# Hybrid decoder layer on one core: the turned tiles of B and x finished apart from their transposition, and the transpositions and stores gathered once a group

## The chip, the cores and the metric

One Trainium2 chip, one of its cores. The time is the device time of one execution in microseconds; of several executions the median is given. The profile is one further execution, taken by the hardware profiler.

## What is computed

A decoder layer with a state-space mixer over 2048 tokens of 1024 features (16 learned tokens stand ahead of them), all in float32:

```python
h = concat([meta, x])
proj = rms_norm(h, norm_mix_w) @ w_in                # [u | z | x B C | dt], 5144 columns
y_pool = pool_mixer(u)                               # 4 trailing means, then a linear map
xbc = silu(causal_dwconv(xBC, conv_w, conv_b))       # 4 taps for each channel
# 24 heads of 64 in 4 groups of 6; B and C (128) are shared by the heads of a group
# in chunks of 128 tokens, S the state that a head carries from chunk to chunk:
y  = ((C B^T) * decay) (x dt) + exp(a_cs) * C S + d_skip * x
S  = S * exp(a_last) + B^T (exp(a_last - a_cs) * x dt)
y  = rms_norm_of_group(y * silu(z)) * ssm_norm_w
h  = h + concat([y_pool, y]) @ w_out
h  = h + relu(rms_norm(h) @ w_ff1)**2 @ w_ff2
out = rms_norm(h, norm_f_w)[:, 16:]
```

## The kernel before

**Blocks.** The 2048 tokens go through the mixer in four blocks b = 0 to 3 of 512 tokens (4 chunks of 128). Block 0 also splits the weights into a high and a low part and stores them; the blocks 1 to 3 load them. After the mixer of a block comes its down projection (line 2031), and after all four the feed-forward part, which makes up the second half of the span. Every product is made of three products of high and low parts.

**The program of each engine** is written out by hand, in order, and engines meet on semaphores alone. In the blocks 1 to 3 the mixer's input products are items: for each group g, B, C, three tiles of x (j = 0, 1, 2, 3, 4: units of 128 columns by 512 tokens, line 1924), then four pieces of the gate z (one for each chunk, 384 columns, line 2011). The items of group 0 come first. Then come 16 steps q = 4 g + c; the step works on chunk c of group g and, between its parts, TensorE makes the items of group g + 1: `mixer_plan` (line 714) gives item n1 at the start of a step and the items n2 later in it, three items in the fourth step and two in the others. The steps of group 3 have no n1 and, from the group's first, one item of the pooling part. So the third step of a group (c = 2) has the last x tile as n1 and the first gate piece as n2, and the fourth (c = 3) has three gate pieces.

**An item** goes from TensorE's bank v % 2 to ScalarE, which evacuates it (`evac`, line 1395, lines 1412 and 1413 for a gate piece; it waits until item v - 2 is finished), to VectorE's taps (line 2467), ScalarE's tanh (line 1447), and VectorE's `finish` (line 2474). TensorE's item v waits until item v - 2 is evacuated (line 1994).

**A step on TensorE** (from line 2207): item n1, transpositions of y of q - 2 (line 2104), diagonal product of q - 1 (line 2116), `slot1` of q (lines 2078 and 2084), state product of q - 1 (line 2134), items n2, and y_offset of q (line 2096). The state product waits for yo of q - 1 on VectorE.

**A step on VectorE** (from line 2642): y of q - 1 (`y_finish`, lines 2565 and 2567), state addition of q - 1 (`state_add`, line 2575), taps of n1, mask (2659), the decay product (2676), B's low part (2682), xdt and xw (2688, 2692), y's low part (2588), xw's low part (2580), the finishes of the pending item and of n1, yo (2705), taps of n2.

**A step on ScalarE** (from line 1597): evacuation of n1, tanh of the pending item, c_both (1608), six falls (1615), the state's high part (1508; in group 3 later), exponential (1621), B's high part (1633), in group 0 the copy of the tokens (1641), squares of y (1534), y's high part (1502), tanh of n1, scaling of y (1518, after GpSimd's root, 1149), xw's high part (1513), evacuation of the items n2. **GpSimd**: low parts of C and of the state (1181, 1185), the root (1148, 1149), ty (1193), the state's carry (1196), ty plus yo (1205).

**Turned tiles.** In group 0 TensorE turns B and x from features by tokens to tokens by features itself (line 2078). For the groups 1 to 3 of the blocks 1 to 3, VectorE turns squares of 32 by 32 within the tile at the end of `finish` (line 2510): B from its tile into `b_turn`, x from `pre` into its own place in F. `store_turned` (line 1385), called at the end of each `evac` for item v - 2, stores the tile to `xt_scr` in HBM, and SP's `load_tokens` (line 846, issues of line 856) brings it back with the squares in their places. F holds two groups' tiles in turn (`group_tile`, line 302).

**SP's queue** (from line 875): for each unit n the weights, 4 units ahead; between them the sums, and at given n the loads of turned tiles and, at n = 16 and 24, the stores of the normalized h of the block before (`store_turned_h`, line 836, four DMAs for each tile t of 128 tokens).

## Time and profile before

| what | us |
| --- | --- |
| median of 3 executions | 2657.96 |
| lowest and highest | 2656.44, 2659.02 |
| the profiled execution | 2655.4 |
| its span | 2653.7 |
| TensorE busy | 2630.8 |
| VectorE, ScalarE, GpSimd busy | 1674.7, 1241.4, 1110.9 |

In the rows PE is TensorE, PEld its weight loads, DVE VectorE, ACT ScalarE, POOL GpSimd, SP the engine that issues most DMAs; ACTq and SPq are the queues' own issues. An operation is named by its line, what it writes and what it reads. A bracket tells how long the engine was idle before it and whose end released it. Times are from the start of the span. The ends of matmuls are modelled, so one overlaps the next; the distance from start to start is what they cost. The granted clock is that of TensorE, 1.00 is 2.4 GHz.

### The profile page before, as it was taken

The page shows a single profiled execution, that of the slowest core. Times are in us where ns is not written, and L with a number is a line of the kernel's source. Part 1 is how long each engine was busy: PE and PEld are TensorE (multiplying, and loading weights), DVE is VectorE, ACT ScalarE, POOL GpSimd, SP SyncE. Part 2 cuts the span into 40 slices and gives each one's busy share as a digit, 9 for nine tenths or more (in the row PEclk, how much of TensorE's full clock was granted, in tenths as well). Part 3 has the DMA queues.
Part 4 walks back from the last instruction along what each step waited for, and adds up shares of the span by engine and source line. Part 5 has one row for each costly group of instructions (what it writes and reads, how often), then busy time and mean ns, then how long its engine had stood idle before and what let it go on. Part 6 is the DMA issues. An engine that isn't in the chain of part 4 may idle for free.

```text
span 2653.7 us, 37407 instructions
## 1 busy us (share of the span) xinstructions
PE 2630.8 (99%) x13818; PEld 2199.1 (83%) x13818; DVE 1674.7 (63%) x2264; ACT 1241.4 (47%) x2474; POOL 1110.9 (42%) x866
## 2 busy tenths in 40 slices
PE   8999999999999999999999999999999999999998
PEld 6888788888888888888888888888888888888887
DVE  6788715888157882478853576564445766666667
ACT  4667653666236662356724455554544222222223
POOL 2133440345004450034544688665555435353434
PEclk9999999999999999999999999999999999999999
DMA  9977676886548866579773655764446742423324
GB/s 333 306 258 244 236 250 247 242 244 220 215 184 264 245 193 235 198 228 253 215 273 138 212 203 198 265 246 142 164 138 236 282 152 101 159 96 127 119 95 159
DMA packets 372739, 551.58 MB, mean 208 GB/s; under 512 B 139450, under 2 KB 240830, under 8 KB 364494
## 3 DMA queue, kind: packets, MB, share of 16 engines
q1 hardware_dynamic: 353550, 539.75, 60.1%
q10 hardware_dynamic: 19008, 9.44, 1.2%
q8 instruction: 110, 1.80, 0.3%
q14 instruction: 71, 0.58, 0.1%
HBM read 393.75 MB, written 155.39 MB: 207 GB/s over the span
## 4 chain that ended last, share of the span: by engine, by line
PE 52%; DVE 1%; DMA 1%; issue 1%; ACT 0%; POOL 0%; SPq 0%; POOLq 0%; ACTq 0%; DVEq 0%
PE bank L2337 22%; PE bank L2305 22%; PE bank L2031 3%; PE bank L1924 3%; PE bank L2011 1%; DMA pair_raw<-T_scr 1%; DVE stage L2812 0%; PE bank L2116 0%; PE bank L2134 0%; PE bank L2096 0%; DVE T_lo L2829 0%; PE bank L2084 0%; PE bank L2104 0%; PE bank L2050 0%; DVE T_lo L2819 0%
## 5 line engine op out<-in xcount | busy, mean ns | idle before, releaser
L1924 PE MATMUL bank<-hnT_hi,w_ring 128*128 128x512 f32 x1152 | 367.6, 391 | 1.6 <-ACT acc L1413 1.6
L2337 PE MATMUL bank<-w_first,T_hi 128*128 128x512 f32 x896 | 275.8, 389 | 0.0
L1924 PEld LDWEIGHTS bank<-hnT_hi,w_ring 128*128 128x128 f32 x1152 | 216.2, 188 | 47.6 <-ACT acc L1413 2.6
L2467 DVE SCALAR_TENSOR_TENSOR acc<-pre,par,acc 128x512 f32<-128x512 f32 x240 | 203.1, 846 | 79.2 <-ACT pre L1428 73.5
L2847 DVE TENSOR_TENSOR acc_th<-bank,acc_th 128x512 f32<-128x512 f32 x224 | 149.9, 685 | 154.1 <-PE bank L2337 153.2
L2305 PE MATMUL bank<-T_hi,w_both 128*128 128x512 f32 x768 | 242.5, 389 | 0.5 <-DVE ff L2788 0.5
L2031 PE MATMUL bank<-w_ring,T_hi 128*128 128x512 f32 x768 | 238.7, 392 | 0.0
L1924 PE MATMUL bank<-hnT_lo,w_ring 128*128 128x512 f32 x576 | 224.5, 390 | 0.0
L2337 PEld LDWEIGHTS bank<-w_first,T_hi 128*128 128x128 f32 x896 | 168.2, 188 | 34.9
L2011 PE MATMUL bank<-w_ring,hnT_hi 128*128 128x384 f32 x768 | 195.9, 335 | 0.6 <-DMA w_ring<-w_scr 0.6
L1924 PE MATMUL bank<-hnT_hi,w_both 128*128 128x512 f32 x544 | 181.9, 405 | 0.2 <-ACT pre L1428 0.2
L2305 PE MATMUL bank<-b,w_both 128*128 128x512 f32 x768 | 179.5, 389 | 0.1
L2337 PE MATMUL bank<-T_hi 128*128 128x512 f32 x448 | 174.4, 389 | 0.6 <-DVE T_lo L2829 0.6
L2337 PE MATMUL bank<-T_hi,T_lo 128*128 128x512 f32 x448 | 174.3, 389 | 0.0
L2337 PE MATMUL bank<-T_lo,T_hi 128*128 128x512 f32 x448 | 174.3, 389 | 0.0
L2337 PE MATMUL bank<-w_first,T_lo 128*128 128x512 f32 x448 | 174.3, 389 | 0.0
L2305 PEld LDWEIGHTS bank<-T_hi,w_both 128*128 128x128 f32 x768 | 144.2, 188 | 31.3 <-DVE ff L2788 1.3
L2305 PEld LDWEIGHTS bank<-b,w_both 128*128 128x128 f32 x768 | 144.0, 188 | 30.3 <-DVE ff L2780 0.5
L2031 PEld LDWEIGHTS bank<-w_ring,T_hi 128*128 128x128 f32 x768 | 142.8, 188 | 28.7
L2305 PE MATMUL bank<-hnT_hi,w_both 128*128 128x512 f32 x512 | 163.2, 389 | 0.0
L1264 POOL TENSOR_TENSOR w_both<-w_sum,w_both 128x512 fp32r<-128x512 f32 x64 | 86.9, 1358 | 181.1 <-ACT w_both L1722 181.1
L1722 ACT ACTIVATE w_both<-w_sum 128x512 fp32r<-128x512 f32 x128 | 80.8, 631 | 173.0 <-PE bank L2305 139.3
(320 smaller groups left out, 6243.1 us busy)
## 6 DMA issues: line engine op xcount, KB each, us to landing
w_ring<-w_scr SPq DMA_DIRECT2D x312, 512.0 KB, 4.7
T_scr<-stage SPq DMA_DIRECT2D x32, 1792.0 KB, 6.6
w_scr<-w_both SPq DMA_DIRECT2D x100, 512.0 KB, 4.3
pair_raw<-in_w_ff SPq DMA_DIRECT2D x36, 1024.0 KB, 5.5
third<-T_scr SPq DMA_DIRECT2D x28, 1024.0 KB, 4.9
pair_raw<-T_scr SPq DMA_DIRECT2D x28, 1024.0 KB, 4.8
sums<-sums_scr SPq DMA_DIRECT2D x64, 384.0 KB, 5.3
raw<-in_w_in SPq DMA_DIRECT2D x36, 512.0 KB, 6.4
```

The source lines that it names most:

```text
L1264: nc.gpsimd.tensor_tensor(lo, left_source(g), hi.bitcast(F32), ALU.subtract).then_inc(w1_lo_pool, 1)
L1722: nc.scalar.activation(hi, left_source(g), ACT.Copy).then_inc(w1_hi, 1)
L1924: mm = nc.tensor.matmul(bank[s][:, :], w[:, k, :], t[:, k, :], start=(k == 0 and j == 0), stop=(k == KT - 1 and j == 2))
L2011: mm = nc.tensor.matmul(bank[s][:, 0:GW].rearrange("p (u c) -> p u c", c=P), t[:, k, tok], w[:, k, :, :], start=(k == 0 and j == 0), stop= ...
L2031: mm = nc.tensor.matmul(bank[4 + t][:, :], a, w[:, kk, :], start=(u == 0 and kk == 0 and j == 0), stop=(u == 7 and kk == 1 and j == 2))
L2305: mm = nc.tensor.matmul(bank1(p, m), w[:, k, :], t[:, k, :], start=(m not in (2, 7, 3) and k == 0 and j == 0), stop=(m not in (1, 6, 5) an ...
L2337: mm = nc.tensor.matmul(bank[4 * half + t][:, :], a[:, k, tok], w[:, k, :], start=(SECOND[q % 7] not in GOES_ON and k == 0 and j == 0), st ...
L2467: ins = nc.vector.scalar_tensor_tensor(acc[:, s, 0:TB], pre[:, s, k:k + TB], w, acc[:, s, 0:TB], ALU.mult, ALU.add)
L2847: ins = nc.vector.tensor_tensor(dst, src, dst, ALU.add)
```

## The change

In the blocks 1 to 3, B's and x's tiles of the groups 1 to 3 are finished in one operation like all others. Their four transpositions stand in a row at the end of the third step of the group before (`x_turning`), in the order B, x, x, x; the turned x goes to the other half of F, where the tiles of the group in work are, and in group 0 waits until TensorE has turned these itself for the last time. The four stores stand in a row in the fourth step, ahead of c_both, each behind its transposition. In the blocks 1 to 3 the state addition stands ahead of y's two operations. The stores of h go out at n = 16 (t = 0, 1), 24 (t = 2) and 32 (t = 3), and y's high parts wait for them accordingly. The load of the next block's x also waits for y of step 14. Whole, but for the context of some parts:

```diff
@@ -314,7 +314,10 @@
         def turn_tile(g, j):
-            return b_turn if j == 0 else group_tile(g, j)
+            return b_turn if j == 0 else group_tile(g + 1, j)
+
+        TURNED = (0, 2, 3, 4)
+        H_STORED_AT = {16: (0, 2), 24: (2, 3), 32: (3, 4)}
         def x_by_pe(b, q):
             return b == 0 or q < CH
@@ -367,6 +370,7 @@
                        for c in range(CH)]
         b_stored = sig("b_stored", 16 * (GROUPS - 1), 0, 0)
         xt_stored = sig("xt_stored", 48 * (GROUPS - 1), 0, 0)
+        x_turned = sig("x_turned_then_w2_loaded2", len(TURNED) * (GROUPS - 1), 0, 0)
         xt_loaded = [sig(f"xt_then_w2_loaded{i}", 64 * (GROUPS - 1), 0, 0) for i in range(2)]
         zc_ps = sig("zc_ps", STEPS)
         z_late = sem("z_late")
@@ -413,7 +417,8 @@
         refill_loaded = [sem(f"refill_loaded{i}") for i in range(3)]
         refill_hi, refill_lo = sem("refill_hi"), sem("refill_lo")
         split_loaded = [sem(f"split_loaded{i}") for i in range(3)]
-        w2_loaded = [xt_loaded[i].sem if i < 2 else sem(f"w2_loaded{i}") for i in range(5)]
+        w2_loaded = [xt_loaded[0].sem, xt_loaded[1].sem, x_turned.sem, sem("w2_loaded3"),
+                     sem("w2_loaded4")]
         w2_sum_ready, w2_hi, w2_lo = sem("w2_sum_ready"), sem("w2_hi"), sem("w2_lo")
         t_loaded = [sem(f"t_loaded{i}") for i in range(2)]
         t_hi, t_lo = sem("t_hi"), sem("t_lo")
@@ -653,7 +658,7 @@
         def w2_arrived(l):
-            return 16 * (l // 5 + 1) + (64 * (GROUPS - 1) * (BLOCKS - 1) if l % 5 < 2 else 0)
+            return 16 * (l // 5 + 1) + (64, 64, len(TURNED), 0, 0)[l % 5] * (GROUPS - 1) * (BLOCKS - 1)
         def w2_source(q):
             c, i = divmod(q, 7)
@@ -898,10 +903,11 @@
                             done = g if j >= 5 else g - 1
                             if after is not None and 0 < done < GROUPS:
                                 load_sums(b, done, after)
-                        if b and n == 24:
-                            hT_stored.wait(sp, b - 1, 128)
-                        if b and n in (16, 24):
-                            for t in (0, 1) if n == 16 else (2, 3):
+                        if b and n in H_STORED_AT:
+                            first, after = H_STORED_AT[n]
+                            if first:
+                                hT_stored.wait(sp, b - 1, 64 * first)
+                            for t in range(first, after):
                                 store_turned_h(b - 1, t)
                         if b and g >= 2 and j == 0:
                             load_tokens(b, g - 1, 0)
@@ -916,6 +922,7 @@
                                 load_tokens(b, GROUPS - 1, 1)
                             if b < LAST and (d, i) == (0, 3):
                                 yoff_ps.wait(sp, b, STEPS)
+                                gated.wait(sp, b, STEPS - 1)
                                 sp.dma_start(xn, x_in[0, (b + 1) * TB:(b + 2) * TB, :].rearrange(
                                     "(t p) d -> p t d", p=P)).then_inc(next_loaded.sem, 16)
                             if (d, i) == (0, 4 if b else 6):
@@ -1382,12 +1389,10 @@
                 steps = Steps(act, act_sem)
-                def store_turned(b, v):
-
-                    n = unit_of(b, v) if b and v >= ITEMS_G else None
-                    if n is None or n >= U_POOL or n % UNITS_G not in (0, 2, 3, 4):
-                        return
-                    g, j = divmod(n, UNITS_G)
+                def store_turned(b, g, k):
+
+                    j = TURNED[k]
+                    x_turned.wait(act, b, len(TURNED) * (g - 1) + k + 1)
                     act.dma_start(xt_scr[b, g, :, j - 2 if j else 3].rearrange("c p n -> p c n"),
                                   turn_tile(g, j).rearrange("p (c n) -> p c n", n=P)
                                   ).then_inc(xt_stored.sem if j else b_stored.sem, 16)
@@ -1397,11 +1402,6 @@
                     s = v % 2
                     ps = bank[s][:, :]
                     up_out.wait(act, b, v - 1)
-                    evacuate(b, v, s, ps)
-                    store_turned(b, v - 2)
-
-                def evacuate(b, v, s, ps):
-
                     piece = piece_of(b, v)
                     if piece:
                         g, c = piece
@@ -1498,6 +1498,8 @@
                     if b and q == CH:
                         hT_stored.wait(act, b - 1, 128)
                     if b and q == 2 * CH:
+                        hT_stored.wait(act, b - 1, 192)
+                    if b and q == 3 * CH:
                         hT_stored.wait(act, b - 1, 64 * CH)
                     nc.scalar.activation(T_hi[:, 4 + 3 * g:7 + 3 * g, c * P:(c + 1) * P],
                                          bank[2][:, 0:GW].rearrange("p (i t) -> p i t", t=P),
@@ -1600,6 +1602,9 @@
                                 high_part(act, N0 + n1 + 2)
                             evac(b, n1)
                             tanh(b, pending)
+                            if b and c == CH - 1:
+                                for k in range(len(TURNED)):
+                                    store_turned(b, g + 1, k)
                         if b:
                             yoff_ps.wait(act, b, q)
@@ -2494,20 +2499,9 @@
                         g, j = divmod(n, UNITS_G)
                         if n >= UNITS_G and j == 0:
                             state_ps.wait(dve, b, (g - 1) * CH if g >= 2 else 0)
-                        if b == 0 or g == 0 or ct is None or j == 1:
-                            nc.vector.scalar_tensor_tensor(group_tile(g, j), pre[:, s, 0:TB], 1.0,
-                                                           acc[:, s, 0:TB], ALU.add, ALU.mult
-                                                           ).then_inc(up_out.sem, 1)
-                            return
-                        dst = group_tile(g, 0) if j == 0 else pre[:, s, 0:TB]
-                        steps.link(nc.vector.scalar_tensor_tensor(dst, pre[:, s, 0:TB], 1.0,
-                                                                  acc[:, s, 0:TB], ALU.add,
-                                                                  ALU.mult))
-                        if j == 0:
-                            sums_stored.wait(dve, b, 16 * GROUPS)
-                        if j == 0 and g > 1:
-                            b_stored.wait(dve, b, 16 * (g - 1))
-                        nc.vector.transpose(turn_tile(g, j), dst).then_inc(up_out.sem, 1)
+                        nc.vector.scalar_tensor_tensor(group_tile(g, j), pre[:, s, 0:TB], 1.0,
+                                                       acc[:, s, 0:TB], ALU.add, ALU.mult
+                                                       ).then_inc(up_out.sem, 1)
                         return
                     i = n - U_POOL
@@ -2539,6 +2533,18 @@
                         hnT_lo[:, k, :], bank[2 + k % 2][:, :],
                         par[:, W_NMIX + k:W_NMIX + k + 1], hnT_hi[:, k, :].bitcast(F32),
                         ALU.mult, ALU.subtract).then_inc(hn_lo.sem, 1)
+
+                def x_turning(b, g, k):
+
+                    j = TURNED[k]
+                    up_out.wait(dve, b, g * ITEMS_G + j + 1)
+                    if k == 0:
+                        sums_stored.wait(dve, b, 16 * GROUPS)
+                        if g > 1:
+                            b_stored.wait(dve, b, 16 * (g - 1))
+                    elif g == 1:
+                        xb_ps.wait(dve, b, CH)
+                    nc.vector.transpose(turn_tile(g, j), group_tile(g, j)).then_inc(x_turned.sem, 1)
                 def h_turning(b, t):
@@ -2660,8 +2666,11 @@
                         if b and n1 is None:
                             masked = mask()
+                        if b and q:
+                            state_add(b, q - 1)
                         if q:
                             y_finish(b, q - 1)
+                        if b == 0 and q:
                             state_add(b, q - 1)
                         taps(b, n1)
                         if b == 0 and n1 is not None:
@@ -2705,6 +2714,9 @@
                         nc.vector.tensor_tensor(by_head(yo[:, :]), by_head(bank[7][:, 0:GW]),
                                                 per_head(ea, c, g), ALU.mult
                                                 ).then_inc(yo_ready.sem, 1)
+                        if b and n1 is not None and c == CH - 2:
+                            for k in range(len(TURNED)):
+                                x_turning(b, g + 1, k)
                         if n1 is None and c >= 2:
                             finish(b, pending - 1)
                         if b == 0 and q < STEPS - 1:
```

## Rows read from the trace of the kernel before

**Rows 1.** The page: busy time of the engines
```profile
PE 2630.8 (99%) x13818; PEld 2199.1 (83%) x13818; DVE 1674.7 (63%) x2264; ACT 1241.4 (47%) x2474; POOL 1110.9 (42%) x866
```

**Rows 2.** Busy time by stretch, block 1's mixer (stretch, length, engines, PEclk, DMA, GB/s)
```profile
465.00:650.00 185.00, 183.87 (x1229) 162.01 (x1227) 152.90 (x249) 121.40 (x331) 88.21 (x106) 1.00 0.79 227
```

**Rows 3.** Waits of TensorE, 460 to 1300 us (total, times, longest)
```profile
PE bank L2134 <- DVE yo L2705: 1.8, 3, 0.6
PE bank L1924 <- ACT acc L1413: 1.6, 3, 0.6
```

**Rows 4.** Three lines of code, all instructions (ns: least/median/most; first, last start)
```profile
L2510 DVE STREAM_TRANSPOSE F<-pre x27: 711/711/716, 480.9 to 1288.9; 128x512 f32<-128x512 f32 x27
L2503 DVE SCALAR_TENSOR_TENSOR pre<-pre,acc x27: 647/678/1322, 480.1 to 1288.2; 128x512 f32<-128x512 f32 x27
L1205 POOL TENSOR_TENSOR ty<-ty,yo x64: 996/1440/1848, 105.8 to 1333.0; 128x384 f32<-128x384 f32 x64
```

**Rows 5.** Timeline of VectorE, block 1, group 0, third step (start, duration)
```profile
486.12 0.56 DVE L2575 TENSOR_TENSOR S<-bank,S 128x384 f32<-128x384 f32 x1 [0.19 <-PE bank L2134]
...
492.03 1.18 DVE L2692 TENSOR_TENSOR xw<-xt,dte 128x384 f32<-128x384 f32 x1
...
494.99 0.71 DVE L2510 STREAM_TRANSPOSE F<-pre 128x512 f32<-128x512 f32 x1
495.63 0.65 DVE L2503 SCALAR_TENSOR_TENSOR pre<-pre,acc 128x512 f32<-128x512 f32 x1
496.31 0.71 DVE L2510 STREAM_TRANSPOSE F<-pre 128x512 f32<-128x512 f32 x1
496.95 0.52 DVE L2705 TENSOR_TENSOR yo<-bank,ea 128x384 f32<-128x384 f32 x1
...
499.71 0.55 DVE L2575 TENSOR_TENSOR S<-bank,S 128x384 f32<-128x384 f32 x1
```

**Rows 6.** Timeline of ScalarE and its DMA queue, group 0, fourth step
```profile
497.06 0.37 ACTq L1391 DMA_DIRECT2D xt_scr<-F  x1
...
497.82 0.31 ACT L1608 ACTIVATE c_both<-F 128x128 fp32r<-128x128 f32 x1
...
500.30 0.52 ACT L1508 ACTIVATE s_both<-S 128x384 fp32r<-128x384 f32 x1 [0.43 <-DVE S L2575]
...
507.17 0.48 ACT L1413 ACTIVATE acc<-bank 128x384 f32<-128x384 f32 x1
```

**Rows 7.** Timeline of TensorE, group 0, third and fourth step
```profile
495.20 0.39 PE L2116 MATMUL bank<-xdt,E 128*64 128x64 f32 x6
...
507.71 0.50 PE L1924 MATMUL bank<-hnT_hi,w_ring 128*128 128x512 f32 x1 [0.54 <-ACT acc L1413]
```

**Rows 8.** Timelines of VectorE, ScalarE, TensorE, block 1, group 1, fourth step
```profile
552.41 0.52 DVE L2705 TENSOR_TENSOR yo<-bank,ea 128x384 f32<-128x384 f32 x1
...
553.27 0.31 ACT L1608 ACTIVATE c_both<-F 128x128 fp32r<-128x128 f32 x1
...
555.76 0.53 ACT L1508 ACTIVATE s_both<-S 128x384 fp32r<-128x384 f32 x1 [0.43 <-DVE S L2575]
...
561.90 0.49 ACT L1413 ACTIVATE acc<-bank 128x384 f32<-128x384 f32 x1
...
562.47 0.47 PE L1924 MATMUL bank<-hnT_hi,w_ring 128*128 128x512 f32 x1
```

**Rows 9.** Timelines of ScalarE and TensorE, block 1, group 2 to 3
```profile
617.74 0.33 ACT L1608 ACTIVATE c_both<-F 128x128 fp32r<-128x128 f32 x1
618.64 1.87 ACT L1615 ACTIVATE E<-sums,acs 128x128 f32<-128x128 f32 x6 [0.56 <-PE bank L2116]
...
624.65 0.60 ACT L1518 ACTIVATE y<-y,small 128x384 f32<-128x384 f32 x1
...
625.31 0.55 PE L2104 MATMUL bank<-ident,y 128*128 128x128 f32 x3
```

**Rows 10.** SP's issues of the loads of turned tiles (ns)
```profile
L856 SPq DMA_DIRECT2D xt<-xt_scr x72: 302/583/5375, 501.5 to 1314.9; - x72
```

## The prediction

> **What bounds the kernel now.** The page first: TensorE is busy 2630.8 us of a span of 2653.7 [rows 1]. The change touches the mixer of the blocks 1 to 3 alone, and the table by stretch shows that of block 1: in 185 us TensorE is busy 183.87 at a granted clock of 1.00, VectorE 152.9, ScalarE 121.4 [rows 2]. Blocks 2 and 3 show the same within 0.02 us. So nothing that makes VectorE's or ScalarE's work less is worth anything in itself. The time moves only where TensorE waits, or where it would newly wait. The list of waits has two such places, three times each, once a block: 0.6 us before the state product (line 2134) for VectorE's yo, and 0.54 us before an input unit (line 1924) for ScalarE's evacuation [rows 3]. With the pipeline's refill they cost about 0.84 and 0.70 us. All that the change could win is therefore 3 x 1.54 = 4.6 us, 0.17%. A measurement of this kernel tells about 0.2%, 5.3 us, from no change.
>
> **The pieces.** I count the mixer's steps from q = 0; four make a group. A transposition of 128x512 takes 0.71 us, a finishing operation 0.68, and 1.32 where it collides with GpSimd; GpSimd's ty takes 1.0 to 1.85 [rows 4].
>
> **1. The finishing operation and the transposition come apart.** The count of instructions stays (36 and 36). Only the wait between the two goes, some 0.04 us each. What moves are four transpositions a group: B's and the first x tile's out of steps with spare VectorE time, and two out of the third step, where they stand ahead of yo. In block 1, group 0 these start at 494.99 and (after 495.63) at 496.31, and yo starts at 496.95 [rows 5]. Start to start a transposition holds the engine 0.64 us (494.99 to 495.63), so yo comes 2 x 0.64 = 1.28 us earlier by this part.
>
> **2. State added first.** In the third step the state addition at 486.12 already waits 0.19 us for its product [rows 5], so it can't come earlier; the two operations of y, which filled that time, now come after it, and the taps and all behind them about 1.1 us later. In group 1 the addition could start some 0.1 earlier, so about 0.95. Against that, the shift takes VectorE partly out of GpSimd's way: nothing to 0.64 us comes back (the 1.32 less the 0.68 of rows 4). I take 0.6, since the slow row of group 1 ends with a GpSimd operation that doesn't move. So yo starts at 496.95 - 1.28 + 1.05 - 0.6 = 496.1. yo ended at 496.95 + 0.52 = 497.47 and TensorE had waited 0.6 us for it, so it was ready at 496.9; yo now ends at 496.6, and this wait is gone. Otherwise the displacement costs nothing: xw, which ended at 492.03 + 1.18 = 493.2, becomes 0.5 to 1.1 later, and TensorE takes it in the diagonal product at 495.20 [rows 7]; in the steps with taps no wait of rows 3 hangs on VectorE. If that margin of 0.9 us went, each us more would go to TensorE. In group 3 the exponential, on ScalarE, ends after y either way.
>
> **3. Four transpositions in a row.** They start about 0.45 us after yo and take 3 x 0.64 + 0.71 = 2.63 us: 496.6 to 499.2. In group 0 the second to fourth also wait for TensorE's own transpositions of the fourth step, whose last is read by about 496.9; B's goes first, to 497.2, and covers that. Behind them wait the state addition (499.71 before, now 499.2) and y. That is early enough.
>
> **4. Four stores in a row on ScalarE's queue, before it goes on.** Here I see the cost. ScalarE now waits for the fourth transposition and issues its store (0.37 us [rows 6]) before c_both, the falls, the exponential and all that depends on them. c_both started at 497.82; now at 499.2 + 0.04 + 0.37 + 0.05 = 499.65, 1.83 later. Of this, 0.43 us was an idle wait for the state addition (500.30) [rows 6], which isn't needed any more. 1.4 us are left, and from the exponential on the chain has no slack for TensorE: squares, GpSimd's root, y's scaling, xw's high part, VectorE's low part, the gate's finish, then the evacuation that ended at 507.17 + 0.48 = 507.65 [rows 6]. TensorE's unit started at 507.71, at once behind it, after a wait of 0.54 [rows 7]; the low part, the gate's finish and GpSimd's root keep their durations. So this start moves to about 509.1: **+1.4 us** net, with both old waits inside it, since an absolute time on ScalarE sets it.
>
> **5. The same in group 1.** yo was at 552.41; with 1.28 less, 0.95 more and 0.64 less it is at 551.45, the transpositions end at 554.5, c_both goes from 553.27 to 555.0, and less the 0.43 wait before 555.76 the chain is 1.3 late. Its evacuation ended at 561.90 + 0.49 = 562.39, and TensorE took it at 562.47 [rows 8]: 0.1 us of slack, where no list of waits shows anything yet. **+1.2 us.**
>
> **6. In group 2** the falls of the next step waited 0.56 us for TensorE anyway (618.64) [rows 9]. c_both at 617.74 + 1.3 = 619.04 puts the falls at 619.24, 0.6 late; y's scaling ended at 624.65 + 0.60 = 625.25 and TensorE took it at 625.31. **+0.5 us.**
>
> **7. The DMA queues.** SP's load of the turned tiles waits for the last store. It was issued at 497.06 and is now at 499.2, with two more ahead of it, and SP's weight loads queue behind those waits. Those wait for the two gate units behind which they stand in any case, and the tokens are first used a unit into the next group, so I take nothing; the cover is the fourth step of a group, and if the loads came later than that, ScalarE's B part would wait. The stores of h over three groups take four of SP's DMAs from n = 24 to n = 32; TensorE reads none of them: nothing, either way. The new wait for gated before the next block's x is met in the same step as, and ahead of, the one that stands there. GpSimd's queue gets no wait; its low parts of C and of the state come later with ScalarE's, still within the two gate units that TensorE has in that step.
>
> **Sum.** 1.4 + 1.2 + 0.5 = 3.1 us a block, 9.3 in three. The profiled execution took 2655.4 us (span 2653.7), so 2664.7 for it; its time is 2.6 us under the median of the runs, 2657.96, to which I add the same: **2667.3**. Bounds: if a store's issue doesn't hold ScalarE (0.37 less) and nothing is given back in part 2 (0.6 more) these nearly cancel; 0.8 us either way at three places in three blocks is 7 us, but not all on one side.
>
> A transposition that meets GpSimd is in no row: all 36 take 0.71. It could take up to 0.64 more, as the finishing operation does; I take nothing, the nearer case: all 36 lie within 5 ns of each other, where the finishing operation, with two inputs in SBUF, spreads from 0.65 to 1.32 [rows 4]. The Trainium skill (SBUF - State Buffer, "Who interferes with whom") says that a VectorE instruction with two SBUF inputs contends with GpSimd's reads; a transposition has one, and by that rule the sum stays.
>
> **Rivals.**
> - **ScalarE isn't held (0.15).** If the four stores are all out by 497.82 + 0.43 = 498.25, the chain starts no later than before. Then the first wait is gone, the state is ready 0.5 us earlier, and the second goes too: -1.54 a block, 2657.96 - 4.6 = 2653.4. This is the case on the other side of no change. It needs the last transposition done by 497.85, 1.35 us before my figure, which two transpositions fewer would give. For it speaks that ScalarE also gets its two evacuations of the third and fourth step 1 us sooner; against it that it has nothing to do with that time but wait.
> - **A milder form (0.20).** The batch ends some 0.7 us earlier than I have it, through GpSimd's collisions, or ScalarE catches up: +0.6, +0.5 and 0 a block: +3.3, 2661.3.
> - **The batch is stretched (0.13).** Each collides with GpSimd's ty: 0.64 more at three places, 9 x 0.64 = 5.8, so 2673.1. Or the fourth store's issue is held by full rings, as SP's turned loads are, whose issue takes 0.58 us but up to 5.4 [rows 10]; 1 us more at the two places beside h's stores is 6 us, about the same.
> - My forecast has 0.52.
>
> **How the numbers follow.** Range 2656 to 2672.5: it takes in my case, the milder one and the lower end of the stretched one, and leaves out most of the first rival. My case alone is 2663 to 2671. Faster by over 0.2% would need more than all the waits there are: 0.04. Slower by over 0.2% (above 2663.3) is most of my case and all of the stretched one: 0.61. The rest, 0.35, is the milder case and most of the first rival.
>
> **What the changed profile would show.** Right: the wait for yo at line 2134 gone; the wait of line 1924 for ScalarE's evacuation at about 2 to 2.6 us at the end of group 0 of each block, and a new one of about 1.2 at the end of group 1; ScalarE idle 2 us or more ahead of c_both in every fourth step, ended by a VectorE transposition; TensorE's idle time in a mixer up by about 3 us. Wrong: c_both less than 0.5 us later than before, or a transposition in the batch above 0.72, or a granted clock below 1.00 behind the longer waits, which would cost more than the waits themselves; before, no wait of TensorE in these stretches is over 0.6 us.

## The result and the profile after

| | before | after |
| --- | --- | --- |
| median, us | 2657.25 | 2685.18 |
| lowest and highest of 4 executions | 2656.44, 2659.02 | 2682.83, 2687.81 |
| the profiled execution, its span | 2655.4, 2653.7 | 2687.81, 2686.1 |

The ratio is 1.0104, with a 95% interval of 1.0087 to 1.0122: 27.9 us slower, where 9.3 were forecast. The profiled execution is the slowest of the four after, 2.6 us above their median; the counts of microseconds below, where they come from the trace, are its own. The page of the changed kernel, to be held against [rows 1]:

```profile
PE 2645.5 (98%) x13818; PEld 2205.6 (82%) x13818; DVE 1685.8 (63%) x2264; ACT 1240.1 (46%) x2474; POOL 1100.6 (41%) x866
```

VectorE and ScalarE issue as many instructions as before. TensorE is busy 15 us more with the same 13818 products, and idle 17.7 more. The list of its waits from 420 to 1360 us tells where the idle time is (total, times, longest; after, for [rows 3]; lines above 1400 have moved by 5 to 9):

```profile
PE bank L1929 <- ACT acc L1413: 16.9, 6, 4.9
PE bank L2109 <- ACT y L1520: 1.8, 3, 0.6
PE bank L2139 <- DVE yo L2714: 1.4, 3, 0.8
PE bank L2101 <- POOL s_both L1192: 1.0, 6, 0.2
PE bank L2016 <- DMA w_ring<-w_scr: 0.4, 1, 0.4
```

The wait for yo in group 0 is gone. The wait of the input unit for ScalarE's evacuation, 0.54 us three times before, is 3.1, 4.9 and 3.4 at the end of group 0 and 1.8 at the end of each group 1. The busy time by stretch tells the rest (columns as in [rows 2]):

```profile
465.00:650.00 185.00, 178.80 (x1169) 156.34 (x1168) 148.22 (x237) 113.87 (x311) 78.36 (x98) 0.99 0.75 223
511.70:515.10 3.40, 3.40 (x9) 2.65 (x8) 0.00 (x0) 0.00 (x0) 0.64 (x1) 0.51 1.02 411
859.90:866.70 6.80, 4.33 (x10) 3.46 (x11) 2.99 (x5) 1.64 (x4) 1.97 (x2) 0.50 1.07 363
```

Behind the long waits TensorE works at a granted clock of 0.50, its level of 1.2 GHz; in block 2 it has already fallen at 859.9, inside the wait that ends at 862.4. Its timeline in block 1 at the end of group 0, after:

```profile
510.93 0.50 PE L1929 MATMUL bank<-hnT_hi,w_ring 128*128 128x512 f32 x1 [3.13 <-ACT acc L1413]
...
513.41 0.63 PE L1929 MATMUL bank<-hnT_lo,w_ring 128*128 128x512 f32 x1
513.84 1.06 PE L1929 MATMUL bank<-hnT_hi,w_ring 128*128 128x512 f32 x2
```

From start to start a product takes 0.43 us there (513.41 to 513.84) where it takes 0.23 elsewhere, so each loses 0.20. Both programs issue the same 13818 products in the same order, so the start of each can be subtracted from its start before. In the three mixers the difference grows by 31.5 us, and the steps of that growth are:

| place | forecast, 3 blocks | measured |
| --- | --- | --- |
| end of group 0, both old waits inside | 4.2 | 2.04 + 3.85 + 2.32 = 8.2 |
| end of group 1 | 3.6 | 1.97 + 1.95 + 1.98 = 5.9 |
| group 2 into 3 | 1.5 | 1.28 + 1.29 + 2.23 = 4.8 |
| products at the lower clock | 0 | 7.6 |
| waits of 0.2 to 0.35 for the state's low part (line 2101) and for yo in groups 1 and 2 | 0 | 3.7 |
| steps too small to name | 0 | 1.3 |

**Group 0, third step, on VectorE** (timeline, after, for [rows 5]; TensorE and with it this stretch lie 1.0 us later than before, from the start-up):

```profile
487.11 0.56 DVE L2581 TENSOR_TENSOR S<-bank,S 128x384 f32<-128x384 f32 x1 [0.15 <-PE bank L2139]
...
492.77 0.95 DVE L2691 TENSOR_TENSOR b_both<-xt,b_both 128x128 fp32r<-128x128 f32 x1
...
493.65 0.55 DVE L2697 TENSOR_TENSOR xdt<-xt,dtt 128x384 f32<-128x384 f32 x1
494.12 1.18 DVE L2701 TENSOR_TENSOR xw<-xt,dte 128x384 f32<-128x384 f32 x1
...
496.36 1.29 DVE L2502 SCALAR_TENSOR_TENSOR F<-pre,acc 128x512 f32<-128x512 f32 x2
497.57 0.55 DVE L2714 TENSOR_TENSOR yo<-bank,ea 128x384 f32<-128x384 f32 x1
498.03 0.70 DVE L2547 STREAM_TRANSPOSE win_tmp<-F 128x512 f32<-128x512 f32 x1
498.66 1.86 DVE L2547 STREAM_TRANSPOSE F<-F 128x512 f32<-128x512 f32 x3
500.44 0.52 DVE L2581 TENSOR_TENSOR S<-bank,S 128x384 f32<-128x384 f32 x1
```

In the clock of before, yo starts at 496.57; I had 496.1. xw is as slow as before (1.18), beside operations of GpSimd. xdt, which took 1.19 before at 490.91, now takes 0.55, but B's low part, 0.28 before at 490.71, takes 0.95: these two cancel. The transpositions, 0.60 apart, end at 499.5 instead of 499.2. All of them, and GpSimd's operation beside the first two (line, engine, ns least/median/most; then a row of GpSimd's timeline):

```profile
L2547 DVE STREAM_TRANSPOSE F<-F x27: 668/669/673, 498.7 to 1321.9; 128x512 f32<-128x512 f32 x27
L2547 DVE STREAM_TRANSPOSE win_tmp<-F x9: 701/702/702, 498.0 to 1320.1; 128x512 f32<-128x512 f32 x9
```

```profile
498.20 1.02 POOL L1212 TENSOR_TENSOR ty<-ty,yo 128x384 f32<-128x384 f32 x1 [3.31 <-DVE yo L2714]
```

ty runs from 498.20 to 499.22, across the transpositions, and none of 36 is stretched. That is the rule which I had cited from the Trainium skill (SBUF - State Buffer, "Who interferes with whom"); here the trace agrees with it.

**The four stores on ScalarE's queue**, group 0 of block 1 and then of block 2, and SP's queue ahead of block 2's (timelines, after, for [rows 6]):

```profile
498.77 0.38 ACTq L1396 DMA_DIRECT2D xt_scr<-win_tmp  x1
499.36 2.15 ACTq L1396 DMA_DIRECT2D xt_scr<-F  x3
501.56 0.31 ACT L1613 ACTIVATE c_both<-F 128x128 fp32r<-128x128 f32 x1 [2.84 <-issue]
```

```profile
848.11 0.42 ACTq L1396 DMA_DIRECT2D xt_scr<-win_tmp  x1
848.70 4.26 ACTq L1396 DMA_DIRECT2D xt_scr<-F  x3
853.01 0.31 ACT L1613 ACTIVATE c_both<-F 128x128 fp32r<-128x128 f32 x1 [4.94 <-issue]
```

```profile
840.45 8.47 SPq L847 DMA_DIRECT2D hT_scr<-h_turn  x8
```

In block 2 the last two issues take 1.97 and 1.62 us instead of 0.37, right after SP's eight stores of h, which it had been issuing until 848.9. c_both, at 838.76 before, starts at 853.01; TensorE's work stood 9.6 us later by then, so it is 4.6 us late instead of my 1.83, and TensorE waits 4.9 us. In group 1, where nothing of h is on the way at that time, the issues are short (0.37 to 0.42):

```profile
559.71 1.60 ACTq L1396 DMA_DIRECT2D xt_scr<-F  x3
561.36 0.31 ACT L1613 ACTIVATE c_both<-F 128x128 fp32r<-128x128 f32 x1 [2.29 <-DVE F L2547]
```

So three things could be behind the 27.9 us: ScalarE held for the fourth transposition (H), VectorE's work put off by the state addition (S), and long issues behind h's stores (Q). The clock would follow from the waits of all three. The experiments take them apart. "Ahead" and "behind" below say whether the four stores stand ahead of c_both or behind the falls.

### The profile page after: what moved, and what is told of

Same layout as the page of the kernel before. It is cut to its first block, busy times and chain, and to the rows that moved or that the text cites. A ratio compares the mean times of both kernels' runs of the same rounds, so it can differ in the third digit from the quotient of the medians.

```text
span 2686.1 us, 37425 instructions
## 1 busy us (share of the span) xinstructions
PE 2645.5 (98%) x13818; PEld 2205.6 (82%) x13818; DVE 1685.8 (63%) x2264; ACT 1240.1 (46%) x2474; POOL 1100.6 (41%) x866
## 4 chain that ended last, share of the span: by engine, by line
PE 83%; DVE 7%; ACT 3%; issue 3%; DMA 2%; POOL 1%; ACTq 0%; SPq 0%; DVEq 0%; POOLq 0%
PE bank L2342 21%; PE bank L2310 21%; PE bank L1929 18%; PE bank L2036 13%; PE bank L2016 2%; DVE acc L2472 2%; PE bank L2121 1%; DMA pair_raw<-T_scr 1%; ACT E L1620 1%; DMA w_scr<-w_both 1%; PE bank L2109 1%; PE bank L2139 1%; DVE F L2502 1%; DVE xw L2701 1%; ACT xw_both L1515 1%
## 5 line engine op out<-in xcount | busy, mean ns | idle before, releaser
L1929 PE MATMUL bank<-hnT_hi,w_ring 128*128 128x512 f32 x1152 | 373.5, 397 | 16.9 <-ACT acc L1413 16.9
L2472 DVE SCALAR_TENSOR_TENSOR acc<-pre,par,acc 128x512 f32<-128x512 f32 x240 | 213.4, 889 | 83.7 <-ACT pre L1428 78.0
L2841 DVE TENSOR_TENSOR T_lo<-third,T_hi 128x1024 fp32r<-128x1024 f32 x56 | 159.4, 2848 | 3.0 <-ACT T_hi L1803 2.8
L1271 POOL TENSOR_TENSOR w_both<-w_sum,w_both 128x512 fp32r<-128x512 f32 x64 | 87.0, 1360 | 181.1 <-ACT w_both L1727 181.1
```

The costliest lines, as they stand in the source:

```text
L1271: nc.gpsimd.tensor_tensor(lo, left_source(g), hi.bitcast(F32), ALU.subtract).then_inc(w1_lo_pool, 1)
L1929: mm = nc.tensor.matmul(bank[s][:, :], w[:, k, :], t[:, k, :], start=(k == 0 and j == 0), stop=(k == KT - 1 and j == 2))
L2472: ins = nc.vector.scalar_tensor_tensor(acc[:, s, 0:TB], pre[:, s, k:k + TB], w, acc[:, s, 0:TB], ALU.mult, ALU.add)
L2841: nc.vector.tensor_tensor(lo[:, k, :], t_raw[x % 2][:, k, :], hi[:, k, :].bitcast(F32), ALU.subtract).then_inc(t_lo, 1)
```

## The experiments

**1. H away, and Q moved behind the falls.** The stores stand behind the six falls, all else as in the change:

```diff
@@ in the step on ScalarE @@
-                            if b and c == CH - 1:
-                                for k in range(len(TURNED)):
-                                    store_turned(b, g + 1, k)
...
                         falls = steps.mark(fall)
+                        if b and n1 is not None and c == CH - 1:
+                            for k in range(len(TURNED)):
+                                store_turned(b, g + 1, k)
```

> The changed kernel, but the four stores stand behind the six falls of the fourth step instead of ahead of c_both. Theory H (ScalarE is held by the four stores): c_both starts again as soon as the evacuation ends, as before the change; the waits of TensorE for ScalarE's evacuation shrink from 2.9 to 4.9 us at the end of group 0 to 0.5 or less, those of 2.0 at the end of group 1 to 0.3 or less, and the granted clock stays at 1.00 in the mixers. What is left are the waits of 0.2 to 0.3 us that the state addition ahead of y makes: 2657 to 2662 us. Rival V (the row of four transpositions on VectorE is itself too long, the stores only stand behind it): the state addition and all behind it stay late, no more than the issues' 0.4 us a place and the long issues come back: 2672 to 2678 us.

Measured: 2663.35 us, ratio 1.0029 [1.0020, 1.0039]. Three quarters of the loss are gone, though it lies 1.3 us above my range. The waits at line 1929 add up to 5.4 us in three (1.2, 2.7 and 1.6 at the end of group 0) instead of 16.9 in six, and the end of group 1 has none. The longest is in block 2, the only place where the clock fell (timeline of ScalarE):

```profile
841.93 1.34 ACTq L1396 DMA_DIRECT2D xt_scr<-F  x1
...
843.32 1.75 ACTq L1396 DMA_DIRECT2D xt_scr<-F  x1
845.12 0.53 ACT L1510 ACTIVATE s_both<-S 128x384 fp32r<-128x384 f32 x1 [2.48 <-issue]
```

The long issues are still there, now over the falls, which ScalarE had been given before; but what comes next in its program, the state's high part, is held. The small waits for the state's low part have stayed too (1.1 us in six).

**2. h's stores moved**, the change else untouched; first two units later, and in a second run one unit earlier:

```diff
-        H_STORED_AT = {16: (0, 2), 24: (2, 3), 32: (3, 4)}
+        H_STORED_AT = {18: (0, 2), 24: (2, 3), 32: (3, 4)}    # 15 in the second
```

> The changed kernel, but the first two tiles of h are stored at n = 18 instead of 16, so behind the row of four stores and not beside it. Theory H with full queues (the third and fourth store of group 0 took 0.58 to 1.97 us to issue because h's 128-byte pieces fill the DMA rings): all four issues take about 0.4 us, the wait at the end of group 0 falls to the 2.0 us of group 1, and the clock falls to half less often: 2671 to 2677 us. Rival (the issues are long for the number of stores in a row, whatever else is under way): no change, 2685 us.

> The changed kernel with the first two tiles of h stored at n = 15 and nothing else. If h's traffic makes the issues of group 0 long: all issues 0.4 us, the three waits at the end of group 0 at 2.0 us like those of group 1, the clock at half in at most two places, and 2672 to 2678 us. At n = 18 the same gave 2679.1 with a new wait of 2.1 us for weights; this should be missing here. Rival (the issues are long for another reason, their number in a row): 2685 us.

Measured: at n = 18 2679.09 us, ratio 1.0084 [1.0067, 1.0101]; at n = 15 2679.4, ratio 1.0086 [1.0071, 1.0102]. Both lie a little above my ranges. In either run all twelve issues of group 0 take 0.37 to 0.42 us, where they took up to 1.97 (timeline of ScalarE's queue, block 2, n = 15):

```profile
847.29 1.60 ACTq L1396 DMA_DIRECT2D xt_scr<-F  x3
```

At n = 15 the waits at the end of group 0 are 2.5, 2.6 and 2.5 instead of 3.1, 4.9 and 3.4 (waits of TensorE, n = 15):

```profile
PE bank L1929 <- ACT acc L1413: 13.1, 6, 2.6
```

At n = 18 they are 2.5 each, but SP, which issues h's stores in front of its weights, brings these late (waits of TensorE from 540 to 552 us, n = 18):

```profile
PE bank L2016 <- DMA w_ring<-w_scr: 2.1, 1, 2.1
```

So it is h's stores that make the issues of group 0 long. Q is worth about 5.8 us by the medians, with what the clock adds, and 4.8 by the ratios, whose intervals meet those of the change; the traces show the effect more surely than the times. It is neither the whole loss nor half of it.

**3. S away.** y stands ahead of the state addition again, the stores stay ahead:

```diff
-                        if b and q:
-                            state_add(b, q - 1)
                         if q:
                             y_finish(b, q - 1)
-                        if b == 0 and q:
                             state_add(b, q - 1)
```

> The changed kernel with y's two operations ahead of the state addition again. Theory D (the state addition first displaces y, the taps and the row of transpositions by about 1 us): the row ends 0.9 us earlier, the waits of TensorE for yo (line 2139) and for the state's low part (line 2101) of 0.2 to 0.3 us go, the three waits of a block for ScalarE are each about 0.9 us shorter, and the clock falls less often: 2670 to 2677 us. Rival (the addition first is worth what it was put there for, the state comes earlier): slower than the changed kernel or equal, 2685 us or more.

Measured: 2669.05 us, ratio 1.0046 [1.0031, 1.0061], a little under my range. The small waits for the state's low part are gone, those for yo too but for one of 0.6 us in block 2, and the waits of group 1 shrink from 1.8 to 0.4, 0.6 and 1.6; those of group 0 stay at 2.6, 3.3 and 3.0. State first costs 2685.18 - 2669.05 = 16 us on top of H and Q.

**4. S alone**, in the kernel before, with its inline transpositions (and the new wait of SP for gated, which holds nothing there):

```diff
@@ kernel before @@
+                        if b and q:
+                            state_add(b, q - 1)
                         if q:
                             y_finish(b, q - 1)
+                        if b == 0 and q:
                             state_add(b, q - 1)
```

> The kernel before, with the state addition ahead of y in blocks 1 to 3 and nothing else (and the wait for y of step 14 ahead of the next block's x, which it then needs). Theory D: the displacement costs small waits and a longer one for yo in the third step of group 0: 2659 to 2664 us. Rival (it costs nothing alone, and all of the loss is the stores'): 2656 to 2658 us.

Measured: 2673.2 us, ratio 1.0062 [1.0047, 1.0077]. I missed this by 9 us. Timeline of VectorE at the end of the third step of group 0, and of TensorE in group 1:

```profile
498.60 0.71 DVE L2511 STREAM_TRANSPOSE F<-pre 128x512 f32<-128x512 f32 x1
499.24 0.52 DVE L2709 TENSOR_TENSOR yo<-bank,ea 128x384 f32<-128x384 f32 x1
```

```profile
557.37 0.79 PE L2135 MATMUL bank<-xw_both,b_both 128*128 128x384 f32 x3 [1.45 <-DVE yo L2709]
```

```profile
PE bank L2135 <- DVE yo L2709: 13.2, 9, 1.5
PE bank L2097 <- POOL s_both L1186: 4.2, 9, 0.6
```

What moves behind the state addition moves yo too, and yo had no slack: before, TensorE already waited for it in group 0. With the transpositions taken out from ahead of yo (part 1) that is covered, without them it is paid nine times. By the same way the state's low part comes late: ScalarE's tanh waits for taps that come later (0.81 us at 547.78 in the trace after), c_both, the falls and the state's high part stand behind it, GpSimd makes the low part of that, and TensorE waits 0.2 to 0.6.

**5. All three away or short: the falls first, y first.** The edits of 1 and 3 together:

> The changed kernel with both causes undone: the four stores behind the falls, y ahead of the state addition. Of the first cause alone undone 7.2 us were left over the kernel before, of the second alone 12.9. If the two causes are all there is: the waits of 0.2 to 0.3 us at lines 2101 and 2139 are gone too, one wait for ScalarE at the end of group 0 stays (the stores' issues are long there), and the time is 2656 to 2660 us against 2656.2 before. Rival (the row of transpositions has a cost of its own, since with y first the state addition of the fourth step comes 1.1 us behind the row's end, the state's high part with it): 2660 to 2664 us, with a wait of about 1 us at the end of groups 0 and 1.

Measured: 2656.85 us, ratio 0.9998 [0.9989, 1.0007]. Nothing of the loss is left, so no further cause is needed; the interval leaves room for at most some 2 us. The transpositions in a row, the other half of F and h's stores over three groups cost nothing together that the times show. They win nothing either: the 0.6-us wait for yo is gone, but the wait at line 1929 is 5.1 us in three.

**6. State first only where ScalarE waits for it**, in the fourth step of the groups 0 to 2, added to 5; then h's first stores at n = 15 as well:

```diff
+                        state_first = b and c == CH - 1 and n1 is not None
+                        if state_first:
+                            state_add(b, q - 1)
                         if q:
                             y_finish(b, q - 1)
+                        if q and not state_first:
                             state_add(b, q - 1)
@@ second run, too @@
-        H_STORED_AT = {16: (0, 2), 24: (2, 3), 32: (3, 4)}
+        H_STORED_AT = {15: (0, 2), 24: (2, 3), 32: (3, 4)}
```

> As the last, but the state addition ahead of y in the fourth step of the groups 0 to 2 alone, where the row of transpositions stands right ahead of it and nothing is displaced. If the addition's place matters only there, this is up to 2 us faster than the last: 2654 to 2658 us. Rival (it matters nowhere once the steps with taps have y first): equal to the last within 1 us.

> As the last, but the first two tiles of h stored at n = 15, a step earlier on SP, so that their small pieces are through before the row of four stores. If what holds the stores' issues in group 0 is h's traffic: four issues of 0.4 us, no wait of TensorE over 0.7 us in the mixers, the granted clock at 1.00 throughout, and 2652 to 2656 us, up to 3 us faster than the kernel before. Rival (h's stores then delay the weights of the gate units, as at n = 18): a wait for w_ring at line 2016 of 1 to 2 us a block, 2658 to 2662 us.

Measured: 2655.8 us, ratio 0.9997 [0.9988, 1.0006], and 2654.27, ratio 0.9989 [0.9980, 0.9997]. In the second TensorE waits for little (waits, 420 to 1360 us):

```profile
PE bank L1929 <- ACT acc L1413: 0.8, 3, 0.3
PE bank L2016 <- DMA w_ring<-w_scr: 0.5, 1, 0.5
```

**7. H alone.** To that version the stores come back ahead of c_both, so that in the third step VectorE has the order of before, and the first tiles of h are out a unit earlier:

```diff
+                            if b and c == CH - 1:
+                                for k in range(len(TURNED)):
+                                    store_turned(b, g + 1, k)
...
                         falls = steps.mark(fall)
-                        if b and n1 is not None and c == CH - 1:
-                            for k in range(len(TURNED)):
-                                store_turned(b, g + 1, k)
```

> The version that came out slightly faster than before (2654.3: stores behind the falls, state added first in the fourth step alone, h's first two tiles at n = 15), with one thing put back: the four stores stand ahead of c_both again. So VectorE does nothing new ahead of the batch, the four issues are short (h's traffic is over), and what is left is ScalarE being held for the fourth transposition. If the hold has a price of its own: c_both about 1.4 to 2 us later in the fourth steps of groups 0 and 1, TensorE's wait for ScalarE's evacuation of the gate piece 1.5 to 2 us at the end of group 0 and up to 1.3 at the end of group 1, about 3 us a block against the version without it: 2660 to 2666. Rival: the whole loss comes from the state addition put first in the third step, which makes the batch late; with the batch on time the hold fits into ScalarE's slack: 2654 to 2657, and no wait above 1 us.

Measured: 2665.84 us, ratio 1.0032 [1.0020, 1.0044], against 0.9989 without H: 0.0043, some 11 us. It is the upper end of what I expected of a price of H's own; the rival, that the batch on time costs nothing, is out. Timeline of ScalarE in group 0 of block 1 (the stretch lies 2.2 us later than before), and the waits:

```profile
498.89 0.38 ACTq L1396 DMA_DIRECT2D xt_scr<-win_tmp  x1
499.77 1.56 ACTq L1396 DMA_DIRECT2D xt_scr<-F  x3
501.38 0.31 ACT L1613 ACTIVATE c_both<-F 128x128 fp32r<-128x128 f32 x1 [2.53 <-DVE F L2547]
```

```profile
PE bank L1929 <- ACT acc L1413: 9.7, 6, 2.2
```

In all three blocks the wait at the end of group 0 is 2.2 us: within the 2 to 2.6 that the prediction had foretold for it. The difference of the starts grows by 0.84, 0.84 and 0.82 there, by 0.56, 0.80 and 2.21 in group 1, by 1.3 in all in group 2, and by 1.5 at the lower clock: in the mixers 8.7 us over the kernel before, where the whole forecast was 9.3. The 2.21 has a long issue in it again, in group 1 of block 3 (timeline of ScalarE):

```profile
1242.09 3.25 ACTq L1396 DMA_DIRECT2D xt_scr<-F  x3
```

The third of the four takes 2.10 us of it, from 1242.68. It isn't h's doing: SP had issued h's third tile from 1235.6 to 1239.1, and the last of its pieces of 128 bytes was through before 1241.5. What the DMA shows beside this issue is the turned stores' own pieces (queue 10) and one packet of program code, 16 KB (the profile's kind "instruction"; DMA of the stretch 1242.5 to 1244.8: packets, MB, share):

```profile
q10 hardware_dynamic: 963, 0.48, 70.8%
q8 instruction: 1, 0.02, 4.9%
```

That packet ended at 1244.37, the issue at 1244.78. The issue of 1.89 us in block 2 at 954.36, ahead of the 1.3 us of group 2, has such a packet beside it too. The last section counts these.

**8. h's stores over two groups**, as before the change, in the version of 6:

```diff
-        H_STORED_AT = {15: (0, 2), 24: (2, 3), 32: (3, 4)}
+        H_STORED_AT = {15: (0, 2), 24: (2, 4)}
```

> The version that came out slightly faster than before (2654.3), with h's tiles 2 and 3 both stored at n = 24, as in the kernel before, and nothing left for n = 32: this is what spreading h's stores over three groups is worth by itself. First theory: nothing, since with the stores of the turned tiles behind the falls a longer issue in group 1 holds only what ScalarE does after the falls, and the traffic of n = 24 ends before them: 2653 to 2656. Rival: twice the traffic at n = 24 stretches the issues in the fourth step of group 1 to over 1 us and holds the state's high part there, 0.5 to 1.3 us more in each of three blocks: 2656 to 2658.5, with a wait of TensorE for ScalarE's evacuation at the end of group 1.

Measured: 2657.59 us, ratio 1.0000 [0.9991, 1.0009]. The interval meets that of 0.9989 [0.9980, 0.9997], so the times alone don't part the two; the traces do, for the rival. Timeline of ScalarE in group 1 of block 1, and its waits:

```profile
554.53 1.44 ACTq L1396 DMA_DIRECT2D xt_scr<-F  x1
...
556.01 1.17 ACTq L1396 DMA_DIRECT2D xt_scr<-F  x1
557.22 0.53 ACT L1510 ACTIVATE s_both<-S 128x384 fp32r<-128x384 f32 x1 [2.28 <-issue]
```

```profile
PE bank L1929 <- ACT acc L1413: 3.7, 6, 1.1
```

With one tile at n = 24 (6, second run) these issues take 0.59 and 0.56 in block 1 and TensorE doesn't wait at the end of group 1. With two it waits 1.1, 1.0 and 0.8 us there. So the tile moved to n = 32 is worth something once the stores stand behind the falls.

**9. The best version once more, and state first taken from it.** The second kernel has y first in the fourth step too:

> The version that came out at 0.9989 of before [0.998, 0.9997], once more, beside one that differs from it in the place of the state addition alone. If its gain is that of TensorE's two waits a block (about 3 to 4.6 us of 2657, as the profile had it in the mixers), the ratio comes out at 0.998 to 0.9995 again, 2652.5 to 2656. Rival: the first value was a lucky placement of the start-up; then 0.9995 to 1.0005.

> The same version with y ahead of the state addition in the fourth step too, so with the order of before in every step: what state first is worth at the only place where ScalarE waits for the state (0.43 us before the state's high part). If the chain from there to TensorE's evacuation of the gate piece has no slack, each of three blocks loses 0.4 us or a little more at the end of group 0 against the version beside it: TensorE's wait for ScalarE's evacuation 0.5 to 1 us instead of 0.3, and 1 to 3 us in all, 2654.5 to 2658. Rival: y, which then comes later with state first, sets the same end through its scaling; then the two are the same within 1 us.

Measured: 2653.59 us, ratio 0.9988 [0.9978, 0.9997], so the small gain came twice; and 2656.52, ratio 1.0002 [0.9993, 1.0011]. The two intervals just meet. Timelines of ScalarE, fourth step of group 0, block 1, the first kernel and then the second:

```profile
501.43 0.52 ACT L1510 ACTIVATE s_both<-S 128x384 fp32r<-128x384 f32 x1 [0.62 <-DVE S L2581]
```

```profile
502.43 0.53 ACT L1510 ACTIVATE s_both<-S 128x384 fp32r<-128x384 f32 x1 [1.68 <-DVE S L2581]
```

State first lets the high part start 1.0 us earlier there, and TensorE's wait at the end of group 0 goes from 1.3 to 0.3 us. Three times 1.0 is the 3 us between the two medians.

## Why the prediction was wrong

The direction was right, and so were the places: ScalarE held by the stores, the wait at line 1929 in groups 0 and 1, the wait for yo gone. What failed was the size: 27.9 us for 9.3, outside the range. By its steps:

- **Part 1** held. 0.60 from transposition to transposition instead of 0.64; they meet no contention.
- **Part 2** failed, in two terms. "I take 0.6" given back by GpSimd's collisions: some 0.15 came (yo at 496.57 where 496.95 - 1.28 + 1.05 is 496.72), because xw stays as slow as it was, and what xdt gains (1.19 to 0.55) B's low part loses (0.28 to 0.95). And "otherwise the displacement costs nothing" was wrong by far the most. I looked only at xw's margin, in group 0. The third step of every group passes its delay on: with the stores ahead, state first costs the 16 us of experiment 3, where I had 0.3 to 0.45 us (0.95 less 0.64, 1.05 less 0.6) at nine places, some 3. In group 1 it makes 0.56 to 0.80 of H into 1.97, and it brings the small waits for yo and the state's low part, 3.7 us.
- **Part 4** had the mechanism, and where H is alone also the size: in block 1 of experiment 7 c_both is 1.4 us late (501.38 less the stretch's 2.2, against 497.82). My 1.83 had 0.45 of part 2 in it, which experiment 7 doesn't have; 1.38 is left. In the same way 1.4 - 0.45 = 0.95 of net loss stands against 0.84, 0.84 and 0.82. Its price of 0.37 for the last issue was the term that failed: 0.87 in block 1 and 1.62 in block 2, behind another of 1.97. I had the 5.4 us of SP's row [rows 10] and put a long issue into a rival of 0.13, with 1 us, instead of into the sum. That full rings are the reason, as I wrote there, no run shows. The stores had been moved next to h's, which I had noted in part 7 only for SP and TensorE.
- **Part 5 and 6**: H alone gave 0.56 and 0.80 where I had 1.2, and in group 2 0 or 1.3 where I had 0.5. Without part 2's 0.31 (0.95 less 0.64) I would have had 0.9 and 0.2. The 2.2 in group 1 of block 3 and the 1.3 each stand behind a long issue. That H alone came to 8.7 us, near my 9.3, is partly luck: for H alone my terms give 3 x (0.95 + 0.9 + 0.2), some 6, and of the 8.7 1.5 us are the lower clock's and about 2.8 those of two long issues, neither of which was in my sum; 4.4 are left.
- **Part 7** held for TensorE: it waits 0.4 us for weights, 0.6 before.
- **The clock** stood only among the signs of being wrong, without a price, although I forecast waits of 2 to 2.6 us, three times longer than any in the trace. It took 7.6 us in the profiled execution. The fastest of the four after, 2682.83, has a mean granted clock of 0.998 where the profiled one has 0.996.

The causes don't simply add. Against the version of 5, at 0.9998, H with Q alone gives +0.0048 (3) and S alone +0.0031 (1), together 21 us; with both the change has +0.0106, 28 us, though Q is in either of the two. The starts in the profiled executions tell where the excess lies, each place as after less 3 less 1: 3.2 us are the clock's (7.6, 2.8 and 1.6), 1.4 stand at the end of group 0 (8.2, 4.7 and 2.1), 2.7 at the end of group 1 (5.9, 3.2 and 0) and 3.2 from group 2 into 3 (4.8, 1.6 and 0). In 3 the 1.6, and 1.8 of the 3.2, stand behind issues of 2.21 and 1.70 us. At the last two places S alone costs TensorE nothing. That there is slack which holds one delay but not two is how I read it; no run tests it.

## What to carry to other kernels

When TensorE is busy 99% of a stretch, an operation put first is paid by all those that it is put ahead of, in each step in which it happens: move it only in the step whose wait names it (here the fourth: 1 us between the medians of 5 and 6, 3 in 9), not in all (16 lost). A DMA issue in the program of a computing engine stands in the order: put it behind the instructions that others wait for, and look at what other queues send at that time, because the issue then takes longer than its row shows. And where a forecast has waits of TensorE longer than any in the trace, give the clock a price.

## What the runs showed of the hardware

- **An issue on ScalarE's queue isn't of constant length, and other queues' traffic is one reason.** With the same store of 128x512 all 84 issues of group 0 take 0.37 to 0.42 us in the seven traces with h's first tiles at n = 15 or 18. In the five with them at n = 16 the longest of each row of four takes 0.73 to 1.99 us, with h's 128-byte pieces moving beside it. Activations that stand ahead of an issue in the program run on meanwhile (experiment 1: the falls); those behind it don't.
- **The other long issues stand beside a packet of program code.** In the traces after and of all experiments but 4, 23 issues take over 0.9 us (0.92 to 2.21, the longest in experiment 3) with no piece of h's moving. All 23 have one of the 16-KB packets of kind "instruction" on queue 8 beside them, and 22 end 0.3 to 0.5 us behind that packet, one 0.9. They are second or third in their row; a row's first issue stays at 0.37 beside such a packet (experiment 9, 1234.13). In experiment 8 this gives 1.42 and 1.79 us in group 2, 50 us behind h's last store. No run moved the packets, so this is a coincidence counted, not a cause tested, and which engine's code it is the trace doesn't tell.
- **After which waits the clock fell.** In the mixers of the traces after and of experiments 1, 2, 3, 5 and 7, TensorE waited 3.0 us or more at line 1929 five times, and five times the granted clock was 0.50 to 0.53 in the stretch behind it, which began from 2.5 us before the wait's end to 1.5 us after it. After 14 waits of 2.0 to 2.7 us it was so five times, after nine of 1.6 to 1.8 once. After the shorter ones never: nine of up to 1.5 in experiment 4, three of 1.3 in 9. So a wait of about 2 us in experiment 7 cost its own length three times, and 1.5 us more the fourth time. What decides between the two isn't settled.
